# A fifth place for split expert weights, SiLU's table on loop entry, and contiguous rows in the expert down pieces

## The reference, cut to what matters

```python
def moe_swiglu(h, router, e_gate, e_up, e_down):
    xt = h.reshape(b * s, d)                            # 256 x 1024
    logits = (xt @ router).astype(jnp.float32)
    top_vals, top_idx = lax.top_k(logits, TOP_K)        # 2 of 8
    w = jax.nn.softmax(top_vals, axis=-1)
    gates = jnp.einsum("nk,nke->ne", w, jax.nn.one_hot(top_idx, N_EXPERTS, dtype=jnp.float32))
    for e in range(N_EXPERTS):
        out = out + gates[:, e:e + 1] * swiglu(xt, e_gate[e], e_up[e], e_down[e])
# swiglu(h, g, u, d) = (silu(h @ g) * (h @ u)) @ d;  g, u: 1024 x 3584;  d: 3584 x 1024
```

## Time and profile before

| | us |
|---|---|
| median of three runs | 1494.33 (1490.82 to 1495.06) |
| profiled execution | 1492.38 |
| its span, first to last instruction | 1490.4 |
| PE busy | 1395.8 (94%) |
| DVE busy | 1174.1 (79%) |
| ACT busy | 1070.0 (72%) |
| expert loop, first matmul to last scaling | 504.5 to 1481.5 |

### The profile page before, as it was taken

How to read it: one execution, slowest core, us unless ns; L and a number is a source line. 1 busy time by engine, 2 the same in 40 slices (tenths; PEclk the granted TensorE clock), 3 DMA queues, 4 the chain that set the end, 5 groups by cost and what they waited for, 6 DMA issues and landing times.

```text
span 1490.4 us, 19309 instructions
## 1 busy us (share of the span) xinstructions
PE 1395.8 (94%) x6469; PEld 1135.6 (76%) x6469; DVE 1174.1 (79%) x1451; ACT 1070.0 (72%) x1372; POOL 119.4 (8%) x181
## 2 busy tenths in 40 slices
PE   6998999997698699999999999999999999999997
PEld 5857788887466588788878878878887887887885
DVE  4785445545694599889989989988988998998996
ACT  4595444446494488887787887888888788788786
POOL 0100000000340610000000000000000000000000
PEclk9999999999799699999999999999999999999998
DMA  9706453212807499999999999999999999999990
GB/s 343 274 11 226 171 204 133 81 44 73 308 2 268 155 347 383 365 361 383 370 359 370 388 355 364 392 351 366 383 384 352 371 377 355 371 386 352 370 364 14
DMA packets 133138, 429.52 MB, mean 288 GB/s; under 512 B 4146, under 2 KB 11485, under 8 KB 133101
## 3 DMA queue, kind: packets, MB, share of 16 engines
q1 hardware_dynamic: 127692, 416.85, 74.8%
q0 software_dynamic: 2624, 9.47, 2.7%
q10 hardware_dynamic: 2784, 2.72, 0.5%
HBM read 422.73 MB, written 6.29 MB: 288 GB/s over the span
## 4 chain that ended last, share of the span: by engine, by line
PE 78%; issue 8%; DVE 7%; ACT 5%; DMA 1%; POOL 0%; ACTq 0%; SPq 0%; DVEq 0%; POOLq 0%
PE bank L576 25%; PE bank L578 24%; PE bank L577 24%; PE bank L540 1%; DVE w_lo L1156 1%; ACT w_hi L783 1%; DMA ring<-in_ev_w_in_dram 1%; DVE w_lo L1226 1%; PE bank L639 1%; ACT h L813 1%; PE bank L667 1%; PE bank L505 1%; ACT gs L803 1%; PE bank L656 1%; ACT w_hi L844 0%
## 5 line engine op out<-in xcount | busy, mean ns | idle before, releaser
L1156 DVE TENSOR_TENSOR w_lo<-ring,w_hi 128x1024 fp32r<-128x1024 f32 x672 | 792.1, 1223 | 74.0 <-ACT w_hi L783 46.0
L783 ACT ACTIVATE w_hi<-ring 128x1024 fp32r<-128x1024 f32 x672 | 702.8, 1063 | 156.1 <-PE bank L578 155.9
L576 PE MATMUL bank<-w_hi,hT_hi 128*128 128x512 f32 (+2 forms) x1264 | 494.2, 391 | 29.8 <-DVE w_lo L1156 13.4
L577 PE MATMUL bank<-w_hi,hT_lo 128*128 128x512 f32 (+2 forms) x1264 | 487.8, 386 | 0.0
L578 PE MATMUL bank<-w_lo,hT_hi 128*128 128x512 f32 (+2 forms) x1264 | 487.6, 386 | 0.0
L576 PEld LDWEIGHTS bank<-w_hi,hT_hi 128*128 128x128 f32 x1264 | 239.4, 189 | 88.1 <-DVE w_lo L1156 22.9
L578 PEld LDWEIGHTS bank<-w_lo,hT_hi 128*128 128x128 f32 x1264 | 239.5, 189 | 47.6
L577 PEld LDWEIGHTS bank<-w_hi,hT_lo 128*128 128x128 f32 x1264 | 239.7, 190 | 44.5
L576 PE MATMUL bank<-w_hi,aT_hi 128*128 128x512 f32 x570 | 227.2, 399 | 10.0 <-issue 5.6
L1226 DVE TENSOR_TENSOR w_lo<-ring,w_hi 128x1024 fp32r<-128x1024 f32 (+3 forms) x124 | 146.2, 1191 | 107.3 <-ACT w_hi L844 107.2
L578 PE MATMUL bank<-w_lo,aT_hi 128*128 128x512 f32 x570 | 223.7, 392 | 0.0
(11 more groups left out here) (237 smaller groups left out, 825.3 us busy)
## 6 DMA issues: line engine op xcount, KB each, us to landing
ring<-in_od_e_gate_dram SPq DMA_DIRECT2D x57, 2048.0 KB, 9.8
ring<-in_od_e_up_dram SPq DMA_DIRECT2D x56, 2048.0 KB, 9.9
ring<-in_od_e_down_dram SPq DMA_DIRECT2D x56, 2048.0 KB, 10.0
ring<-in_ev_w_gate_dram SPq DMA_DIRECT2D x5, 2048.0 KB, 7.7
ring<-in_ev_w_up_dram SPq DMA_DIRECT2D x5, 2048.0 KB, 7.7
ring<-in_ev_w_down_dram SPq DMA_DIRECT2D x5, 2048.0 KB, 8.0
ring<-in_ev_w_in_dram SPq DMA_DIRECT2D x4, 2048.0 KB, 19.9
ring<-in_ev_w_out_dram SPq DMA_DIRECT2D x2, 2048.0 KB, 19.0
```

Source lines behind the costliest of these rows:

```text
L576: pe.matmul(dst, hi, whi, start=first, stop=False)
L577: pe.matmul(dst, lo, whi, start=False, stop=False)
L783: act.activation(w_hi[:, (NQ + q) % SPLITS, :], ring[:, i % RING, j * QUARTER:(j + 1) * QUARTER], ACT.Copy).then_inc(hi_ready, 1)
L1156: dve.tensor_tensor(w_lo[:, place, :], ring[:, i % RING, j * QUARTER:(j + 1) * QUARTER], w_hi[:, place, :].bitcast(F32), ALU.subtract).the ...
```

## The change

It does four things.

1. A fifth place. The right half of `hT_hi` and `hT_lo` becomes place 4 for split expert weights. `E_PLACES` gives the place of each of the 84 quarters of a slot: 0 to 4 in turn, except that the 36th to the 39th quarter take 0 to 3 and the next starts at 0 again (84 is no multiple of 5). ACT and DVE split quarter q + 4 in step with quarter q (AHEAD), four quarters are split ahead of the loop, and ACT waits for the last use of the same place.
2. A SiLU of one column is computed ahead of the loop, before the gathered rows are taken.
3. Down pieces are loaded with four consecutive rows of `e_down` for each partition (`(p k)` in place of `(k p)`): 16 KB in one run. Quarter j then multiplies rows 4p + j, so `turn` transposes every fourth column of `y` (step 4, four offsets) in place of a block of 128.
4. Weights and output banks are addressed as blocks of 128 columns, so that both kinds of place have one form: four blocks for TensorE, eight for ACT and DVE.

```diff
+E_PLACES = 7 * (0, 1, 2, 3, 4) + (0, 1, 2, 3) + 9 * (0, 1, 2, 3, 4)
+AHEAD = 4
...
+def place_of(q):
+    return E_PLACES[q % len(E_PLACES)]
+
+
+def same_place_before(q):
+    return max(r for r in range(q - len(E_PLACES), q) if place_of(r) == place_of(q))
...
+        e_hi_at = [w_hi[:, p, :].rearrange("p (a n) -> p a n", a=8) for p in range(SPLITS)]
+        e_hi_at += [hT_hi[:, :, CAP:2 * CAP]]
+        e_lo_at = [w_lo[:, p, :].rearrange("p (a n) -> p a n", a=8) for p in range(SPLITS)]
+        e_lo_at += [hT_lo[:, :, CAP:2 * CAP]]
...
-                        "o (k p) n -> p (o k) n", p=P)
+                        "o (p k) n -> p (o k) n", p=P)
...
-            sp.wait_ge(lo_ready, slots * EQ + (NQ + 4 * (1 - RING)))
-            load(0, 0, *order[0])
+            for i in range((AHEAD + 3) // 4):
+                sp.wait_ge(lo_ready, slots * EQ + (NQ + 4 * (i + 1 - RING)))
+                load(0, i, *order[i])
...
+            def out(b):
+                return bank[b][:, :].rearrange("p (a n) -> p a n", a=4)
...
-                    at = m * NW
-                    wh, wl = w_hi[:, place, at:at + NW], w_lo[:, place, at:at + NW]
+                    wh, wl = (at[place_of(q)][:, 4 * m:4 * m + 4, :] for at in (e_hi_at, e_lo_at))
...
-                                              y[:, part * NW + b * P:part * NW + (b + 1) * P], ident)
+                                              y[:, part * NW + b:(part + 1) * NW:4], ident)
...
+            act.activation(rt[:, 1:2], eps[:, 0:1], ACT.Silu)
             take_gathered(1)
-            for q in range(LEAD - 1):
-                if q == 0:
-                    act.wait_ge(arrived[0], 16 * (uses[0] + 1))
-                act.wait_ge(quarter_used, NQ + q - SPLITS + 1)
-                act.activation(w_hi[:, (NQ + q) % SPLITS, :], ring[:, 0, q * QUARTER:(q + 1) * QUARTER], ACT.Copy)\
+            act.wait_ge(quarter_used, NQ)
+            for q in range(AHEAD):
+                i, j = q // 4, q % 4
+                if j == 0:
+                    act.wait_ge(arrived[i], 16 * (uses[i] + 1))
+                act.activation(e_hi_at[q], eights(ring[:, i, j * QUARTER:(j + 1) * QUARTER]), ACT.Copy)\
                    .then_inc(hi_ready, 1)
...
-                    act.wait_ge(quarter_used, s * EQ + (NQ + q - SPLITS + 1))
-                    act.activation(w_hi[:, (NQ + q) % SPLITS, :], ring[:, i % RING, j * QUARTER:(j + 1) * QUARTER],
+                    act.wait_ge(quarter_used, s * EQ + (NQ + same_place_before(q) + 1))
+                    act.activation(e_hi_at[place_of(q)], eights(ring[:, i % RING, j * QUARTER:(j + 1) * QUARTER]),
                                    ACT.Copy).then_inc(hi_ready, 1)
...
-                        split(4 * i + j + LEAD - 1)
+                        split(4 * i + j + AHEAD)
```

More of the change, by code:

```diff
@@ L513, in quarter @@
                 j = q % 4
-                place = (NQ + q) % SPLITS
                 pe.wait_ge(lo_ready, s * EQ + (NQ + q + 1))
                 for m in range(2):
-                    at = m * NW
-                    wh, wl = w_hi[:, place, at:at + NW], w_lo[:, place, at:at + NW]
+                    wh, wl = (at[place_of(q)][:, 4 * m:4 * m + 4, :] for at in (e_hi_at, e_lo_at))
                     if kind == "down":
                         half = slice((4 * part + j) * P, (4 * part + j + 1) * P)
-                        mm = three(bank[4 + m][:, :], eT_hi[:, half], eT_lo[:, half], wh, wl,
+                        mm = three(out(4 + m), eT_hi[:, half], eT_lo[:, half], wh, wl,
                                    c == 0 and part == 0 and j == 0, c == NCH - 1 and j == 3)
@@ L525, in quarter @@
                         b = 2 * (kind == "up") + m * (CHUNKS[c] == 2)
-                        mm = three(bank[b][:, :], hT_hi[:, k, 0:CAP], hT_lo[:, k, 0:CAP], wh, wl,
+                        mm = three(out(b), hT_hi[:, k, 0:CAP], hT_lo[:, k, 0:CAP], wh, wl,
                                    k == 0, k == KD - 1)
@@ L740, in _, with eights @@
             experts_pe(pe, three, turn_norm)
+        def eights(ap):
+            return ap.rearrange("p (a n) -> p a n", a=8)
         def experts_act(act, norm):
@@ L1145, in experts_dve @@
             take_gathered(1)
-            for q in range(LEAD - 1):
+            for q in range(AHEAD):
+                i, j = q // 4, q % 4
                 dve.wait_ge(hi_ready, NQ + q + 1)
-                place = (NQ + q) % SPLITS
-                dve.tensor_tensor(w_lo[:, place, :], ring[:, 0, q * QUARTER:(q + 1) * QUARTER],
-                                  w_hi[:, place, :].bitcast(F32), ALU.subtract).then_inc(lo_ready, 1)
+                dve.tensor_tensor(e_lo_at[q], eights(ring[:, i, j * QUARTER:(j + 1) * QUARTER]),
+                                  e_hi_at[q].bitcast(F32), ALU.subtract).then_inc(lo_ready, 1)
             with dve.Fori(0, slots) as s:
@@ L1153, in split @@
                     i, j = q // 4, q % 4
-                    place = (NQ + q) % SPLITS
                     dve.wait_ge(hi_ready, s * EQ + (NQ + q + 1))
-                    dve.tensor_tensor(w_lo[:, place, :], ring[:, i % RING, j * QUARTER:(j + 1) * QUARTER],
-                                      w_hi[:, place, :].bitcast(F32), ALU.subtract).then_inc(lo_ready, 1)
+                    dve.tensor_tensor(e_lo_at[place_of(q)], eights(ring[:, i % RING, j * QUARTER:(j + 1) * QUARTER]),
+                                      e_hi_at[place_of(q)].bitcast(F32), ALU.subtract).then_inc(lo_ready, 1)
                 def turned(c):
```

## The result

The changed kernel takes 1477.43 us in the median of five runs (1477.14 to 1483.26), the kernel before 1494.33 in the median of five (1490.82 to 1499.66); the ratio is 0.990 (95% interval 0.987 to 0.993). Timed again beside others (label a_again), it took 1477.0 against 1496.3, ratio 0.986 (0.984 to 0.988). The forecast of 1475.1 us was 2.3 us short of it, and the range of 1470 to 1487 held.

A forecast was written before the change was run, and what follows sets the result against it. The expert loop was taken as bound by TensorE, with only its gaps to win: 7 x 2.63 = 18.4 us plus 0.8 in slot 0, together 19.2, so 1494.3 - 19.2 = 1475.1 us; range 1470 to 1487 (8 in 10).

The forecast's parts named there:

- three gaps a slot: TensorE waits for w_lo at a slot's fourth, twelfth and twentieth quarters: 1.70, 0.47 and 0.13 us late, 2.63 with restarts.
- the restart: First matmul after each of TensorE's gaps lasts 0.50 instead of 0.39 us: 0.11 more each, 0.33 a slot.
- Slot 0: First slot of the expert loop, entered from the prologue without the first gap: 0.6 + 0.2 = 0.8 us won.
- The fifth place: Expert loop: 1.36 us more in hand; wins 0.24 at quarter 20, 0.58 at quarter 12; its row reads taken as free.
- SiLU's table: SiLU ahead of the loop removes both table loads in each slot; with the fifth place the first gap's 1.81 us is won.
- rival 1: Table loads stay in the loop; fifth quarter late in seven slots, costing 3.2 us: 1478; chance 0.10.
- The strided read: The 28 transposes a slot in turn load y with a step of four words; cost taken as nothing, bound 67 us.
- Rival 2: TensorE's new reads cost something, up to doubling stationary loads, 0.10 x 224 = 22 us: 1475 to 1497; chance 0.19.
- Rival 3: Strided load of y takes four times as long: 1542; slower than before once a transpose costs 0.09 us more; chance 0.07.
- The down rows: Down pieces arrive as 16 KB rows, landing in about 10 us as before; faster landing wins nothing.
- Rival 4: Down pieces land more slowly in large rows; costs from 1.6 us a piece, 1680 at twice 5.3 us; chance 0.04.
- the 25 us in hand: Spare time of a down piece in the ring: wanted 35 us after its place is refilled, landing in 10.0 us.

The follow-up runs named there:

- a_no_silu: Changed kernel without the SiLU ahead of the loop; median 1482.3 us, ratio 0.991 to the kernel before, slot 119.93 us.
- b_silu_only: Kernel before with only the SiLU ahead of the loop added; median 1482.8 us, ratio 0.991, slot 119.93 us.
- a_turn_steps: Changed kernel with extra transposes of steps two and eight ahead of each four of the turn; 0.118 and 0.113 us each, step four 0.120, flat 0.109.
- a_detour1: Changed kernel with one copy of 128 x 1024 on ACT ahead of each slot's first split; slot 119.47 us, run once.

## Why the prediction was right, point by point

- **What bounds the loop.** TensorE with three gaps a slot for want of `w_lo`: right. In the changed kernel they are gone, and where an edit was undone they came back at the quarter named and, within 0.1 us, at the size named (a_no_silu, b_silu_only).
- **The sizes.** 2.63 us a slot were forecast, 2.53 measured; 19.2 for the loop against 18.0. Two terms were off, with opposite signs. The transposes' step was taken as nothing and costs 0.28 a slot (119.34 against 119.06), 2.2 us in all. What the gaps cost was taken 0.18 too low (2.63 + 0.18 - 0.28 = 2.53). That the two nearly cancel is luck. Half of the 0.18 is the restart, which I took as 0.11 from the first matmul's length: the eighteen steps after the gap of the earlier trace rows take 880.61 - 876.38 = 4.23 us, 0.15 more than at the undisturbed pace, and those after the other two gaps 0.13 each more. Another 0.04 is a fourth gap, which the prediction overlooked. Before, in the first quarter of the last down piece:

```profile
864.21 0.69 DVE L1163 TENSOR_TENSOR aT_lo<-bank,aT_hi 128x512 fp32r<-128x512 f32 x1
...
864.74 0.39 PE L578 MATMUL bank<-w_lo,aT_hi 128*128 128x512 f32 x1
865.03 0.49 PE L576 MATMUL bank<-w_hi,aT_hi 128*128 128x512 f32 x1
...
880.61 0.39 PE L576 MATMUL bank<-w_hi,hT_hi 128*128 128x512 f32 x1
```

  The step of 0.29 ends just after DVE's `aT_lo` of the last turn, for which TensorE waits there in the code. The wait isn't for a place, and half of it is still there in the changed kernel (862.97 - 862.71 = 0.26). The last 0.05 of the 0.18 isn't traced.
- **Slot 0.** From its first matmul to its first scaling it took 627.1 - 504.5 = 122.6 us before and 630.2 - 507.7 = 122.5 in the changed kernel: 0.1 won in place of 0.8. The steps of the transposes took 0.28 of that. The rest goes with the clock, which the sum left out: the loop opens at 1.2 GHz, a granted clock of 0.50 and steps of 0.43 us, until about 509 before and 513.4 here. In the tables of stretches:

```profile
505.00:508.90 3.90, 3.90 (x10) 3.00 (x10) 3.14 (x4) 3.50 (x4) 3.41 (x7) 0.50 0.00 0
...
508.00:513.30 5.30, 5.30 (x13) 4.13 (x13) 5.30 (x5) 3.30 (x5) 4.98 (x5) 0.50 0.20 45
```

  That opening lasts from 3.1 to 6.1 us in the runs here, whatever the kernel.
- **The fifth place.** Its four rows of 128 cost TensorE nothing. A quarter from that place keeps the pace of the earlier trace rows, six steps in 875.32 - 873.96 = 1.36 us, and the view of line 592 in the changed kernel has the same median length for its matmuls (`bank<-hT_hi`) as for the others:

```profile
L592 PE MATMUL bank<-w_hi,aT_hi x474: 387/389/796, 195.4 to 1463.3; 128*128 128x512 f32 x158
L592 PE MATMUL bank<-hT_hi x160: 388/389/477, 516.0 to 1442.6; 128*128 128x512 f32 x160
...
873.96 0.39 PE L592 MATMUL bank<-hT_hi 128*128 128x512 f32 x1
...
875.32 0.39 PE L592 MATMUL bank<-w_hi,hT_hi 128*128 128x512 f32 x1
```

- **SiLU's table.** Both loads of a slot went, so rival 1 did not come about. Its price was 7 x 0.59 = 4.1 us by a_no_silu, not 3.2: the fifth quarter came 0.42 late, not 0.34, and restarts cost more.
- **The strided read.** Rival 2 came about at a tenth of its bound: 0.012 us a transpose, not 0.10. Rival 3, the slower side, would have needed 0.09. The argument for nothing, that a load reads its words at half a stream's pace, came nearer than a doubling but isn't shown: the cost isn't nothing, and in a_turn_steps it doesn't follow the groups of four words. The Trainium skill's page "SBUF — State Buffer", section "Door 1: The DMA port swizzle", asks for two hits in a line of 16 bytes and calls a step of four fp32 free. It fits no better: a step of two has two hits in a line and still costs 0.009, and the step of four costs 0.011.
- **The down rows.** No loss in landing: 9.9 against 10.0 us, and in the two pairs that differ by the rows alone 0.3 and 0.6 us earlier. TensorE never waited for a piece, so that won nothing. Rival 4 had no occasion; the 25 us in hand weren't tried.
- **The medians.** The two comparisons gave 16.9 and 19.2 us against 19.2 forecast. The prediction's own range of 1472 to 1478 is wider at the top than its source, since the spread of the three runs carried over ends at 1495.1 - 19.2 = 1475.9. The part ahead of the loop moves by up to 9 us between executions (loop starts from 502.5 to 511.9), more than any of the smaller terms.

## What to carry to other kernels

Read a loop's gaps from the starts of the bound engine, find for each the detour of the feeding engine, and set the detour's length against what is in hand: that gave each gap's size to 0.1 us, and it told that two remedies for one detour (a deeper buffer, a detour made shorter) don't add up. A function whose table a loop needs can be called once ahead of the loop; that one line, alone, won 1.94 us a slot where the whole change won 2.53. A layout that makes transfers neater is worth nothing while pieces land long before they are wanted, and its price may stand on another engine.

## What the runs showed of the hardware that I had not expected

- Four fp32 transposes whose stationary operand is read with a step take 0.45 to 0.48 us against 0.44 flat, and their loads are recorded at some 190 to 212 ns against 140. Steps of two, four and eight words hardly differ, and the largest was the cheapest.
- After a gap TensorE lost 0.13 to 0.15 us over the next matmuls, 0.11 of it at the first step (0.34 us in place of 0.23).
- A matmul whose weights come just in time loses 0.1 us though the timeline lists no idle time for it (a_detour1: 753.84 to 754.17 in place of 0.23).
- In the same attention stretch the granted clock was 1.00 in some executions and 0.72 to 0.89 in others, with no order by kernel.
